# The context stream goes first at each layer and perceptron of a two-block transformer kernel

## The reference

```python
for l in range(DEPTH_2):                      # 2 layers
    last = l == DEPTH_2 - 1
    sa, ca, ga, sm, cm, gm = ada_params(c_lat, w_ada[l], b_ada[l])
    sa_c, ca_c, ga_c, sm_c, cm_c, gm_c = ada_params(c_cx, w_ada[l], b_ada[l])
    h = modulate(rms_norm_2(x, g_mix[l]), sa, ca)
    hc = modulate(rms_norm_2(ctx, g_mix[l]), sa_c, ca_c)
    u, q, k, v = split_heads(h @ w_in[l])
    uc, qc, kc, vc = split_heads(hc @ w_in[l])
    ...                                       # attention and pooling -> mix
    x = x + ga * (mix @ w_out[l])
    x = x + gm * sq_relu_mlp(modulate(rms_norm_2(x, g_mlp[l]), sm, cm), w_mlp1[l], w_mlp2[l])
    if not last:
        ctx = ctx + ga_c * (mix_c @ w_out[l])
        ctx = ctx + gm_c * sq_relu_mlp(modulate(rms_norm_2(ctx, g_mlp[l]), sm_c, cm_c), ...)
return rms_norm_2(x, g_final)
```

## Time and profile before

| what | value |
|---|---|
| median of 3 runs | 2817.89 us (2817.3 to 2821.45) |
| the profiled execution's own time | 2822.84 us |
| span of the profiled execution | 2821.1 us |
| mean granted PE clock | 0.974 of full |
| PE busy | 2640.1 us, 94% of the span |
| DVE busy | 1623.8 us, 58% |
| ACT busy | 886.1 us, 31% |
| HBM read | 239.31 MB, 86 GB/s over the span |

### The profile page before, as it was taken

One profiled execution on the slowest core, in us unless ns is written; L12 is line 12 of the kernel. 1 busy time (PEld: TensorE's weight loads), 2 busy tenths in 40 slices (PEclk: granted clock), 3 DMA queues, 4 the chain that ended last, 5 costly groups with the idle time before them and its releaser, 6 DMA issues.

```text
span 2821.1 us, 47956 instructions
## 1 busy us (share of the span) xinstructions
PE 2640.1 (94%) x20452; PEld 2147.4 (76%) x20452; DVE 1623.8 (58%) x2743; ACT 886.1 (31%) x1488; POOL 128.7 (5%) x215
## 2 busy tenths in 40 slices
PE   6999978888999899998999999999999898999997
PEld 3777667877788788887777778888888776788886
DVE  3455558888634578885367455545454466544434
ACT  3444410000222522333255342213132345323322
POOL 0000012222000000000000000000000000000000
PEclk9999999999999999998999999999999999999999
DMA  6100420000122344441100203233432100332220
GB/s 263 34 27 31 162 102 3 3 3 3 70 99 111 120 169 189 179 164 56 48 13 31 105 31 118 99 105 120 142 135 90 41 31 31 126 113 90 90 90 30
DMA packets 25155, 244.49 MB, mean 87 GB/s; under 512 B 2832, under 2 KB 2992, under 8 KB 9840
## 3 DMA queue, kind: packets, MB, share of 16 engines
q1 hardware_dynamic: 12960, 181.61, 16.9%
q0 software_dynamic: 11984, 59.81, 6.3%
HBM read 239.31 MB, written 2.10 MB: 86 GB/s over the span
## 4 chain that ended last, share of the span: by engine, by line
PE 87%; DVE 8%; issue 2%; ACT 2%; DMA 1%; DVEq 0%; ACTq 0%; POOLq 0%
PE ps L338 55%; PE ps L1289 7%; PE ps L1919 2%; PE ps L2148 2%; PE ps L944 1%; PE ps L367 1%; PE ps L2176 1%; PE ps L2192 1%; PE ps L368 1%; PE ps L369 1%; PE ps L900 1%; PE ps L2194 1%; PE ps L2193 1%; DMA raw<-in_w_ada 1%; PE ps L946 1%
## 5 line engine op out<-in xcount | busy, mean ns | idle before, releaser
L338 PE MATMUL ps<-hh,ws 128*128 128x512 f32 x3216 | 751.1, 393 | 15.1 <-DVE hh L519 7.5
L338 PEld LDWEIGHTS ps<-hh,ws 128*128 128x128 f32 x3216 | 601.7, 188 | 148.7 <-issue 19.0
L321 ACT ACTIVATE ws<-raw 128x1024 fp32r<-128x1024 f32 x295 | 309.0, 1050 | 467.8 <-PE ps L338 428.5
L329 DVE TENSOR_TENSOR ws<-raw,ws 128x1024 fp32r<-128x1024 f32 x295 | 359.8, 1222 | 163.6 <-ACT ws L321 163.6
L338 PE MATMUL ps<-g,ws 128*128 128x512 f32 x1536 | 364.1, 395 | 0.0
L338 PEld LDWEIGHTS ps<-g,ws 128*128 128x128 f32 x1536 | 286.3, 188 | 66.7
L1289 PE MATMUL ps<-ar 64*64 64x64 f32 x6656 | 227.9, 227 | 13.2 <-DVE ar L1411 7.3
L1289 PEld LDWEIGHTS ps<-ar 64*64 64x64 f32 x6656 | 214.6, 142 | 33.3 <-DVE ar L1411 10.4
L338 PE MATMUL ps<-gg,ws 128*128 128x512 f32 x960 | 226.1, 396 | 0.0
L1598 DVE SCALAR_TENSOR_TENSOR xT<-ps,mods,xT 128x512 f32<-128x512 f32 x120 | 90.0, 750 | 220.4 <-PE ps L338 212.2
L338 PEld LDWEIGHTS ps<-gg,ws 128*128 128x128 f32 x960 | 180.2, 188 | 43.8 <-DVE gg L1739 0.4
(11 more groups left out here) (357 smaller groups left out, 3396.9 us busy)
## 6 DMA issues: line engine op xcount, KB each, us to landing
raw<-in_w_m SPq DMA_DIRECT2D x32, 2048.0 KB, 8.1
raw<-in_w_mlp SPq DMA_DIRECT2D x16, 2048.0 KB, 8.3
raw<-in_w_ada SPq DMA_DIRECT2D x12, 2048.0 KB, 9.6
...
```

The costliest lines, as they stand in the source:

```text
L321: e.activation(w_of(n)[0], pieces[n][2], ACT.Copy).then_inc(*hi(n))
L329: e.tensor_tensor(l, pieces[n][2], h.bitcast(F32), ALU.subtract).then_inc(*lo(n))
L338: m = e.matmul(o, a, b, start=n == 0, stop=n == 3 * kt - 1)
```

## The change

In the two convolution tiles before attention 1, each query tile is rotated before the context's half of the tile, and DVE writes the masks before the first of them.

In the second block the context goes first wherever a layer or a perceptron begins. Its input is loaded before `mlp0`; its squares, its stats and its norm for layer 0 are made beside `mlp0`, in given pieces (`scalar_beside0`, `vector_beside0`, `tensor_beside0`), with `lam` for both layers. At the other heads the context is normed first and multiplied first, and its stats are taken in the middle of the last tile's `x` product (`middle`). The gains are made behind the last modulation job. For this the modulation jobs are spread in another way (`share`): for layer 0 over pieces 8 to 55 (three slots of one tile), for layer 1 two jobs a piece and one in every fourth from piece 8 on, which ends at piece 44; it keeps its one slot. What runs beside a perceptron is now done behind each piece's own work, and no longer ahead of it. Regions of SBUF are laid out anew for it.

```diff
-        def product(e, o, lhs, rhs, kt, name, ready=None):
+        def product(e, o, lhs, rhs, kt, name, ready=None, middle=None):
             n = 0
             for k in range(kt):
+                if middle is not None and k == kt // 2:
+                    middle()
                 if ready is not None:
                     e.wait_ge(*dve[ready, k])
                 (lh, ll), (rh, rl) = lhs(k), rhs(k)
...
                 for t in ps.take(name):
                     e.wait_ge(*t)
-                product(e, ps[name][:, 0:w], lhs, rhs, kt, name, ready)
+                product(e, ps[name][:, 0:w], lhs, rhs, kt, name, ready, middle if i == len(groups) - 1 else None)
...
-        def act_norm(e, tag, bv, dst, bufs):
...
 
-        def dve_norm(e, tag, x, r, av, bv, dst, bufs, stats=None):
+        def dve_norm(e, *args):
+            for _ in dve_norm_steps(e, *args):
+                pass
+
...
-                pe_conv(e, i)
+                _, n, m, _, _, _ = convs[i]
+                of_x, of_c = streams(n, m, True)
+                pe_tile(e, 7 + i, [of_x])
                 pe_head_turn(e, ("q", 2 + i), T, qa[:, 2 + i, :], "perm1", dve[("q", 2 + i), "scaled"])
+                pe_tile(e, 7 + i, [of_c])
                 if i == 0:
                     pe_head_sum(e, ("q", 3), T, sq[:, 0, :])
...
             for i in range(2):
-                if i == 1:
+                dve_head_turn(e, ("q", 2 + i), T, qa[:, 2 + i, :], cs1, rs[:, :])
+                split_lo(e, min(7 + i + 2, 18))
+                if i == 0:
                     dve_head_scale(e, ("q", 3), qa[:, 3, :], qg8, sq[:, 1, :])
-                dve_head_turn(e, ("q", 2 + i), T, qa[:, 2 + i, :], cs1, rs[:, :])
+                    dve_masks(e)
                 dve_conv_tile(e, i)
...
-            split_lo(e, min(7 + i + 2, 18))
...
-        def vector_attention(e):
+        def dve_masks(e):
             e.wait_ge(*lo[final[load_before["att"]]])
             e.tensor_copy(mb[:, 0, :], C("ident")).then_inc(*dve())
             e.tensor_copy(mb[:, 1, :], C("mprev")).then_inc(*dve())
             e.tensor_copy(mb[:, 2, :], C("mnext")).then_inc(*dve("mb"))
             e.tensor_scalar(nsink, Q("sink"), -1.0, None, ALU.mult).then_inc(*dve("nsink"))
+
+        def vector_attention(e):
             split_lo(e, 11)
...
+        def pe_row_stat(e, tag, row):
+            j, _, _, _, w, bufs, bank = row
+            pe_stat(e, (*tag, j), w, bufs, (bank,))
...
+                for t in range(48):
+                    if t >= n:
+                        e.wait_ge(*dve["modulated", l, last_of[t - n]])
+                    e.dma_start(w[t % n], I["w_ada2"][l][:, t, :]).then_inc(*wada_in[t % n]((l, t), 16))
...
+                for _ in range(3):
+                    yield
+                todo = list(enumerate(jobs))
+                for piece in range(8, 64):
+                    for i, (t, j) in todo[:share(piece)]:
+                        e.wait_ge(*wada_in[t % n][l, t])
+                        e.wait_ge(*dve["modulated", l, jobs[i - 1]] if i else dve[tag])
+                        e.tensor_tensor_reduce(junk, w[t % n], cb[:, j * 1024:j * 1024 + 1024], 1.0,
+                                               Q2("bada", l)[:, t:t + 1], ALU.mult, ALU.add,
+                                               mods[:, 1 + l, t, j:j + 1]).then_inc(*dve(("modulated", l, (t, j))))
...
+                            dve_gains2(e, l)
+                    todo = todo[share(piece):]
+                    yield
...
+        def dve_gains2(e, l):
+            md = mods[:, 1 + l, :, :]
+            e.wait_ge(*dve["mods", l])
+            dve_gain(e, A1, md, 1, 0, Q2("gmix", l))
+            dve_gain(e, A1c, md, 1, 1, Q2("gmix", l))
...
+            by_size = rows_[::-1]
...
+                beside = aside[3](e) if aside and len(aside) > 3 else iter(())
+                for j, h, hid, x, w, bufs, bank in by_size:
...
+                        next(beside, None)
...
                     for m in range(8):
+                        next(beside, None)
+                        end = q == 3 and m == 7
                         pe_tile(e, start("d", q) + m,
                                 [((tag, "d", q, m, j), of(hid), w, (tag, "hid", q, j) if m == 0 else None)
-                                 for j, h, hid, x, w, bufs, bank in rows_])
+                                 for j, h, hid, x, w, bufs, bank in (by_size if end else rows_)],
+                                middle=(lambda: pe_row_stat(e, (tag, "s"), rows_[1])) if end and len(rows_) > 1 else None)
                         if q == 2 and m == 7:
                             ps.use = range(8 - len(rows_))
-                for j, h, hid, x, w, bufs, bank in rows_:
-                    pe_stat(e, (tag, "s", j), w, bufs, (bank,))
+                pe_row_stat(e, (tag, "s"), rows_[0])
...
-        mod_l0 = modulation(0, ar[:, 9216:13312], 2, ar[:, 13312:17408], 2)
-        mod_l1 = modulation(1, ada_slot, 1, ada_slot[:, 3072:4096], 1)
-        mlp0 = mlp_streams("m0", mod, [(0, hh, gg, xT, T, SQX, 7)], mod_l0)
+
+
+        mod_l0 = modulation(0, ar[:, 9216:13312], 3, ar[:, 13312:16384],
+                            lambda n: 0 if n >= 56 else (2, 2, 2, 3)[n % 4] if n // 8 % 2 else (2, 1, 2, 2)[n % 4])
+        mod_l1 = modulation(1, ada_slot, 1, ada_slot[:, 3072:4096], lambda n: 2 if n % 4 else 1)
+        rs_c2 = ar[:, 8192:8448]
+        bufs_c2 = [ar2[:, 11264 + 256 * i:11520 + 256 * i] for i in range(4)]
+        CS, CN = ("c2", "s"), ("c2", "n")
...
+        def tensor_beside0(e):
+            for _ in range(20):
+                yield
+            pe_stat(e, CS, TC, SQC)
+            for t in ps.take("lam"):
+                e.wait_ge(*t)
+            e.wait_ge(*dve["lam"])
+            e.matmul(ps["lam"][:, 0:4], ones[:, :], lam, start=True, stop=True).then_inc(*acc("lam"))
...
+            act_rms(e, CS, TC, rs_c2)
+            e.wait_ge(*acc["lam"])
...
+            for _ in range(36):
+                yield
+            for k in range(KT):
+                act_norm(e, CN, shift_c2, hc2, bufs_c2, [k])
+                if k % 2:
+                    yield
+
+        def vector_beside0(e):
+            norm = dve_norm_steps(e, CN, ctx2, rs_c2, lambda k: col(A1c, k), shift_c2, hc2, bufs_c2, CS)
+            for n, _ in enumerate(mod_l0[2](e)):
+                if 11 <= n < 17:
+                    dve_square_sum(e, CS, n - 10, SQC)
...
+                if 57 <= n < 62:
+                    for _ in range(3 if n == 57 else 2):
+                        next(norm, None)
+                yield
+
+        beside0 = mod_l0[0], scalar_beside0, vector_beside0, tensor_beside0
+        mlp0 = mlp_streams("m0", mod, [(0, hh, gg, xT, T, SQX, 7)], beside0)
...
+            e.dma_start(ctx2[:, :, :], I["ctxT2"]).then_inc(*come["cx2"]("in", 16))
...
-            def tensor_head(e):
...
                 split_hi(e, tile_piece[l, "u", 3] + 2)
                 if l:
-                    e.wait_ge(*acc[(before, "s", 0), "st"])
                     act_rms(e, cs, TC, rsc2)
+                    act_norm(e, tc, shift(1), hc2, bufs_c2, range(0, 3))
                 act_rms(e, xs, T, rs[:, :])
-                meet(e, act, (l, "before"))
-                e.wait_ge(*acc[l, "lam"])
-                e.activation(l2, ps[l, "lam"][:, 0:2], ACT.Exp).then_inc(*act((l, "lam")))
+                if l:
+                    act_norm(e, tc, shift(1), hc2, bufs_c2, range(3, KT))
                 act_norm(e, tx, shift(0), hh, bufs_x2)
-                if l == 0:
-                    e.wait_ge(*dve[tx, KT - 1])
-                    e.wait_ge(*come["cx2"]["in"])
-                    for k in range(KT):
-                        act_square(e, cs, k, ctx2[:, k, :], rms_bufs(TC))
-                    act_rms(e, cs, TC, rsc2)
-                act_norm(e, tc, shift(1), hc2, bufs_c2)
 
             def vector_head(e):
                 split_lo(e, tile_piece[l, "u", 3] + 2)
-                meet(e, dve, (l, "before"))
-                lv_ = Q2("lam", l).rearrange("p (i q) -> p i q", i=2)
-                e.tensor_tensor(l2, lv_[:, :, 0], lv_[:, :, 1], ALU.mult).then_inc(*dve((l, "lam")))
+                if l:
+                    dve_norm(e, tc, ctx2, rsc2, lambda k: col(A1c, k), shift(1), hc2, bufs_c2, cs)
+                dve_norm(e, tx, xT, rs[:, :], lambda k: col(A1, k), shift(0), hh, bufs_x2, xs)
...
+            def gpsimd_head(e):
                 e.wait_ge(*dve["mods", l])
-                dve_gain(e, A1, md, 1, 0, Q2("gmix", l))
-                dve_gain(e, A1c, md, 1, 1, Q2("gmix", l))
-                dve_gain(e, A2, md, 4, 0, Q2("gmlp", l))
-                if not last:
...
-                e.tensor_tensor(nlam, mi[:, 3:4], mi[:, 2:3], ALU.subtract).then_inc(*dve())
-                e.wait_ge(*dve.prev())
-                e.tensor_scalar(nlam, nlam, -lam_init, None, ALU.add).then_inc(*dve((l, "nlam")))
```

(52 more changed lines are left out.)

138 lines of the change are left out of this document (67 added, 71 removed).

## The result

The changed kernel takes 2825.68 us, the kernel before 2820.51 in the same rounds (medians of 18 runs each); the ratio is 1.0018, with a 95% interval of 1.0009 to 1.0026. The interval lies above 1, so it is slower by 0.1 to 0.3%; the forecast was 2813.1, faster by 0.2%. The execution profiled has a span of 2825.0, 3.9 longer than before.

A forecast was written before the change was run, and what follows sets the result against it. PE, busy 94% of the span, was taken as the bound. Gains of 6.0 + 16.5 + 3.3 + 1.0 = 26.8 less 22 for modulation 1 gave -4.8: 2817.9 to 2813.1 us, range 2794 to 2826.

The forecast's parts named there:

- head of layer 0: From E, the end of the stage's last tile, to `v`: 31.2 us instead of 47.8; net gain 16.5 us.
- perceptron head: Start of layer 0's perceptron: context normed and multiplied first, x's tiles done at E + 23.0; gain 3.3 us.
- head of layer 1: From E (end of the last tile) to `v` in layer 1: 33.6 us instead of 34.6, gain 1.0.
- the start of the scores: Attention 1: first scores start at 137.65, not 141.86, 4.2 us earlier; moving the masks alone would bring 0.45.
- Rival 1: Layer 0's perceptron: modulation 1's single slot costs PE nothing; 2791 us, or 2802 with half the ledger; chance 0.15.
- Rival 2: Modulation 1's round trips lengthen when asked for more often: gains gone at 4.65 us, 2826 at 4.9; chance 0.16.
- rival 4: The heads and attention 1 give less: 2823 us at worst, about 2818; chance 0.10.
- nothing lost there but the 0.7: First perceptron, `mlp0`: three slots suffice; only 0.7 us lost as PE's piece 20 waits for DVE's last work in piece 18.
- the ledger of modulation 1: Layer 0's perceptron: DVE's lateness from the single slot's round trips, summed piece by piece; PE loses 22 us.
- The estimate of 9 us for this loss: Modulation 1's loss if weights landed in the skill page's 3.2 us instead of the trace's 3.8; kernel at 2800.
- Attention 1: Gain 6.0 us: scores 4.2 earlier plus 1.8 of PE clock; bounds 0.45 and 9.5.
- Rival 3: PE's clock survives shorter gaps: attention 1 gives 9.5 us, head of layer 0 1.5 more; 2808 us; chance 0.15.

The follow-up runs named there:

- a_xfirst: Changed kernel with x first again, in norm and tiles, where the perceptron of layer 0 begins: 2827.99 us, ratio 1.0033 to the kernel before.
- a_share: Changed kernel with modulation 1 thinned out to one job a piece, two in every fourth: 2801.04 us, ratio 0.9937 to the kernel before.
- b_dense: Kernel before with modulation 1's new density alone, two jobs a piece and one in every fourth: 2853.41 us, ratio 1.0121.
- a_ahead: Changed kernel with the extra work in layer 0's perceptron ahead of each piece's own work again: 2834.27 us, ratio 1.0045 to the kernel before.
- a_square: Changed kernel with ScalarE's squares of the context in the first perceptron one piece later: 2816.76 us, ratio 0.9992 to the kernel before.
- a_best: Changed kernel with modulation 1 thinned out, its second slot from tile 16, and ScalarE's squares one piece later: 2787.93 us, ratio 0.9888 to the kernel before.
- a_bank: a_best with the bank ring of layer 1 moved on by one, as it stood before: 2785.17 us, ratio 0.9867 to the kernel before.

## Why the prediction was wrong, point by point

**What was right.** Every mechanism of the sum was there, and most sizes: head of layer 0 (`v` at E + 31.4 for 31.2), perceptron head (third tile 4.3 nearer to E for 4.2, of which a_xfirst gives 3.7 to the order), head of layer 1 (2.0 for 1.0), the start of the scores (137.94 for 137.65) and what they wait for, no gain from the masks, and modulation 1 as a thing that takes much of it back, where and in what pattern. Rival 1 fell with a_share and b_dense. Rival 2, longer trips, did not decide in after: 4.33 in the mean of 32 against 4.29 assumed (it may in a_ahead and b_dense). Its prices were too low: by the ledger, worked through again, 27 us are lost at a trip of 4.5, not 4.65, and 33 at 4.7, not 4.85; the 34 at 4.77 fits these. Of rival 4 nothing came.

**The step that failed: "In `mlp0` there are three slots, and no piece averages above PE's 5.5: nothing lost there but the 0.7".** I counted VectorE's work per piece and the slots, and left out the order in which two engines wait for each other. The stats of the context made a ring of ScalarE and VectorE that idles VectorE by 1.43 in each of six pieces. It cost 8.3 (a_square); the stage was 6.2 longer than before instead of 1.7. The miss of 4.5 would have been larger still, but for the 3.0 of the old wait, which I had overlooked, and the 0.7, which did not come: 8.3 - 3.0 - 0.7 = 4.6. That part is luck. The rows of before could not show the new ring, but the diff could: count in which piece square k, sum k - 1 and the next split are issued, and the square turns out to be one piece early.

**The term that was mis-sized: the ledger of modulation 1, 22 for 25.9.** Its waits were even a little too high (21.8 for 18.6). What it left out is the clock: behind waits of 2.63, 3.09 and 8.28 TensorE ran at 0.77, 0.77 and 0.68, 6.5 more. I had counted low clock behind gaps at the heads, and not behind the waits that I was adding. It should have been a term. The Trainium skill (page TensorE: Matmul & The Clock Gate, section HAM oscillation — how this bites in real kernels) describes a loop whose waits for transfers lower the clock of the work behind them. These rows agree in kind, but the wait of 2.63 is shorter than those of its example. The estimate of 9 us for this loss, worked out from a figure of the Trainium skill (page DMA: Bandwidth & Descriptors, section Anatomy of one DMA — SWDGE (gpsimd) path), is refuted by the 18.6 of waits alone.

**Attention 1: 6.0 forecast, 7.0 in the profiled execution.** By the gates it is 4.4 in after and 4.9 in the mean of the ten traces, so of the clock part, 1.8, some 0.2 to 0.7 came there. By `x2` the mean is 7.8, and what the edit has to do with the rest is open. Rival 3 (9.5 here and 1.5 more at the head of layer 0) is not borne out by after; but in a_square, a_best and a_bank the head of layer 0 did give these 1.5, with the same gaps.

**Left out: 1.3 us in layer 1**, 0.7 of it the ring of banks (a_bank) and 0.3 the lower clock of the first 12 `v` matmuls (3.36 for 3.02); **and the order of m1's extra work**: with it ahead the stage took 5.7 more (a_ahead, cause open). The 25.9 already has the better order.

In all: +4.5 in mlp0 and +3.9 in m1, +1.3 at the end, against 1.0 more at attention 1, 1.0 more at layer 1 and 1.0 less in the two rows of layer 0 between: -4.8 + 4.5 + 3.9 + 1.3 - 1.0 - 1.0 + 1.0 = +3.9, the span's own difference.
